# Pauses between GpSimd's pieces, pooled sums behind the key norm, a branch gate multiplied in PSUM, and dense portions around two softmaxes

## The reference

```python
h = rms_norm(x, n1)
z = jnp.einsum('bld,de->ble', h, w_in)
... # o_gla, o_hgrn: chunked linear attention; o_pool: trailing-window means
q = rms_norm(heads(nq, H_D), q_ng)
kv_slc_new = jnp.stack([rms_norm(heads(sk, KVH_D), k_ng[1]), heads(sv, KVH_D)], axis=2)
kv_win_new = jnp.stack([rms_norm(heads(wk, KVH_D), k_ng[2]), heads(wv, KVH_D)], axis=2)
... # NSA: three attentions (compressed, selected, window) with a gate for each
return gb[..., 0:1] * o_cmp + gb[..., 1:2] * o_slc + gb[..., 2:3] * o_win
...
proj = jnp.einsum('blnc,ncd->blnd', branches, w_branch)
gate = jax.nn.sigmoid(jnp.einsum('bld,de->ble', h, w_gate) + b_gate)
x = x + jnp.einsum('bld,de->ble', jnp.sum(gate * proj, axis=2), w_out)
u = jax.nn.relu(jnp.einsum('bld,df->blf', rms_norm(x, n2), w1))
x = x + jnp.einsum('blf,fd->bld', u * u, w2)
```

## Time and profile before

| | us |
|---|---|
| median of 3 runs | 1301.05 |
| lowest and highest | 1300.05, 1306.36 |
| profiled execution, its own time | 1310.57 |
| span in its trace | 1308.7 |
| PE busy | 1225.1 (94%) |
| DVE, POOL, ACT busy | 657.4, 585.0, 345.8 |
| mean granted clock of PE | 0.977 |

### The profile page before, as it was taken

One profiled execution on the slowest core, in us unless ns is written; L12 is line 12 of the kernel. 1 busy time (PEld: TensorE's weight loads), 2 busy tenths in 40 slices (PEclk: granted clock), 3 DMA queues, 4 the chain that ended last, 5 costly groups with the idle time before them and its releaser, 6 DMA issues.

```text
span 1308.7 us, 23691 instructions
## 1 busy us (share of the span) xinstructions
PE 1225.1 (94%) x10261; PEld 1159.6 (89%) x10261; DVE 657.4 (50%) x1036; ACT 345.8 (26%) x516; POOL 585.0 (45%) x433
## 2 busy tenths in 40 slices
PE   4989999999887888899998989989999999999999
PEld 4989899887787778788897988889999999999998
DVE  6244666535475546766755533237387500477200
ACT  5231222210531224333322121223232211222210
POOL 1424566211336338866533434224555544455442
PEclk9999999999998989999998998999999999999999
DMA  4320112123322233434342325142232222233232
GB/s 193 107 72 33 65 66 65 34 69 94 105 65 80 85 113 114 177 114 162 113 156 71 129 85 190 50 146 87 77 113 83 96 97 87 92 97 93 86 97 98
DMA packets 42908, 129.30 MB, mean 99 GB/s; under 512 B 3958, under 2 KB 15006, under 8 KB 40621
## 3 DMA queue, kind: packets, MB, share of 16 engines
q1 hardware_dynamic: 38197, 102.62, 24.1%
q0 software_dynamic: 4608, 25.17, 5.4%
HBM read 121.64 MB, written 6.36 MB: 98 GB/s over the span
## 4 chain that ended last, share of the span: by engine, by line
PE 84%; DVE 9%; DMA 3%; issue 2%; ACT 1%; SPq 0%; POOL 0%; DVEq 0%; ACTq 0%
PE PS L622 20%; PE PS L624 19%; PE PS L623 19%; PE PS L651 9%; PE PS L934 2%; PE PS L727 2%; DMA M<-w_tiles 2%; PE PS L912 2%; PE PS L922 1%; PE PS L1087 1%; DMA M<-state_hgrn 1%; PE PS L763 1%; PE PS L765 1%; DVE stat L1903 1%; PE PS L1079 1%
## 5 line engine op out<-in xcount | busy, mean ns | idle before, releaser
L2195 POOL TENSOR_TENSOR WL<-M,WH 128x512 fp32r<-128x512 f32 x314 | 431.9, 1400 | 647.1 <-ACT WH L1216 646.6
L622 PE MATMUL PS<-hH,WH 128*128 128x260 f32 x1360 | 403.0, 296 | 16.8 <-DVE M L1503 6.6
L624 PE MATMUL PS<-hH,WL 128*128 128x260 f32 x1360 | 389.5, 286 | 0.0
L623 PE MATMUL PS<-hL,WH 128*128 128x260 f32 x1360 | 389.2, 286 | 0.0
L622 PEld LDWEIGHTS PS<-hH,WH 128*128 128x128 f32 x1360 | 261.8, 193 | 32.5 <-issue 27.9
L1216 ACT CAST WH<-M 128x1024 fp32r<-128x1024 f32 x159 | 166.1, 1047 | 378.6 <-DMA M<-w_tiles 243.6
L623 PEld LDWEIGHTS PS<-hL,WH 128*128 128x128 f32 x1360 | 262.2, 193 | 0.4
L624 PEld LDWEIGHTS PS<-hH,WL 128*128 128x128 f32 x1360 | 261.8, 192 | 0.0
L624 PE MATMUL PS<-uH,WL 128*128 128x260 f32 x512 | 144.7, 283 | 0.0
L622 PE MATMUL PS<-uH,WH 128*128 128x260 f32 x512 | 144.6, 282 | 0.0
L623 PE MATMUL PS<-uL,WH 128*128 128x260 f32 x512 | 144.1, 282 | 0.0
(11 more groups left out here) (368 smaller groups left out, 1981.5 us busy)
## 6 DMA issues: line engine op xcount, KB each, us to landing
M<-w_tiles SPq DMA_DIRECT2D x159, 512.0 KB, 3.5
M<-x_T SPq DMA_DIRECT2D x8, 520.0 KB, 5.9
M<-cache_win_kv SPq DMA_DIRECT2D x2, 2048.0 KB, 10.3
y_T<-M SPq DMA_DIRECT2D x8, 260.0 KB
con<-tables SPq DMA_DIRECT2D x1, 1475.5 KB, 12.4
M<-state_gla SPq DMA_DIRECT2D x2, 512.0 KB, 6.6
M<-state_hgrn SPq DMA_DIRECT2D x2, 512.0 KB, 10.4
gla_sample<-M SPq DMA_DIRECT2D x2, 512.0 KB, 6.0
```

The costliest lines, as they stand in the source:

```text
L622: mm(out, hi[:, cols], x_hi, start=first, stop=False)
L623: mm(out, hi[:, cols], x_lo, start=False, stop=False)
L624: return mm(out, lo[:, cols], x_hi, start=False, stop=last_k)
L2195: last = p.tensor_tensor(WL8[s][:, c], WR[s][:, c], WH8[s][:, c], ALU.subtract)
```

## The change

Five things. `lower` on POOL waits for its first piece before it issues the second, and for the second before anything else. The pooled sums begin behind `tick("nsa", 8)` and wait for `k_norm`. In `att` the reciprocal and the gate are no longer multiplied with each other (128x8); the gate is multiplied into PSUM in an instruction of its own (128x512). `cmp` gets three ticks more, 13 of 5, which PE issues behind the scores and ahead of the wait for `cp`. Each softmax round gets a third tick, on PE ahead of the wait for r1, on DVE ahead of the wait for the exponentials. The table pays for it: `att` 3.8 triples in a tick, `s6` 58 ticks of 5.15.

```diff
-SECTIONS = (... ("nsa", 22, 5), ("cmp", 10, 5),
-            ("att", 68, 4), ("s6", 56, 5.4))
+SECTIONS = (... ("nsa", 22, 5), ("cmp", 13, 5),
+            ("att", 68, 3.8), ("s6", 58, 5.15))
...
# PE, compressed scores
                     tick("cmp", 3 + i // 2)
+            for i in range(5, 8):
+                tick("cmp", i)
             pe.wait_ge(*done("cp"))
...
-                tick("cmp", 5 + i)
+                tick("cmp", 8 + i)
...
# PE, sums_of_round
                 tick("s6", at + 1)
+                tick("s6", at + 2)
                 pe.wait_ge(sem("r1"), n + 1)
...
# DVE, compressed softmax
             step(v.tensor_reduce(nmc, cm, AX, ALU.max, negate=True))
+            tick("cmp", 5)
             v.tensor_tensor(cm, cm, bc(nmc, 32), ALU.add).then_inc(once("cm"), 1)
+            tick("cmp", 6)
             dve.wait_ge(*done("cm_e"))
...
+            tick("cmp", 7)
             step(v.reciprocal(rsc, rsc))
...
# DVE, att
                     step(v.reciprocal(rs[:, i, b], rs[:, i, b]))
-                    step(v.tensor_tensor(rs[:, i, b], rs[:, i, b], gate[:, i, :, 1 + b], ALU.mult))
...
                     step(v.tensor_tensor(t, t, bc(rs[:, i, b], HD), ALU.mult))
+                    step(v.tensor_tensor(t, t, bc(gate[:, i, :, 1 + b], HD), ALU.mult))
...
# DVE, softmax_of_round
+                tick("s6", at + 2)
                 dve.wait_ge(sem("sxe"), 2 * n + 2)
...
# POOL, lower
-                    last = p.tensor_tensor(WL8[s][:, c], WR[s][:, c], WH8[s][:, c], ALU.subtract)
-                last.then_inc(sem("w_lo"), 1)
+                    ins = p.tensor_tensor(WL8[s][:, c], WR[s][:, c], WH8[s][:, c], ALU.subtract)
+                    if i == 0:
+                        step(ins)
+                ins.then_inc(sem("w_lo"), 1)
+                gp.wait_ge(sem("w_lo"), n + 1)
...
# POOL, pooled sums
-            for i in range(5):
+            for i in range(9):
                 tick("nsa", i)
+            gp.wait_ge(*done("k_norm"))
             gp.wait_ge(sem("dv"), FREED[U_DONE][1])
```

More of the change, by code:

```diff
@@ L167 @@
 FREED = evacuations()
-SECTIONS = (("prep", 10, 7), ("lev", 32, 7.5), ("dec", 14, 5), ("ssl", 7, 5), ("smp", 24, 5), ("nsa", 22, 5), ("cmp", 10, 5),
-            ("att", 68, 4), ("s6", 56, 5.4))
+SECTIONS = (("prep", 10, 7), ("lev", 32, 7.5), ("dec", 14, 5), ("ssl", 7, 5), ("smp", 24, 5), ("nsa", 22, 5), ("cmp", 13, 5),
+            ("att", 68, 3.8), ("s6", 58, 5.15))
 FIRST, CUM, _sum = {}, [], 0
@@ L585, in _ @@
                              zn[0:NS, 4, col:col + 256]).then_inc(sem("rows_out"), 16)
-            for i in range(10):
+            for i in range(13):
                 tick("cmp", i)
@@ L597, in _ @@
                              [:, 4 * n:4 * n + 4]).then_inc(sem(f"xw{n}"), 16)
-            for i in range(56):
+            for i in range(58):
                 tick("s6", i)
@@ L1055, in _ @@
             sums_of_round(0, SN[1], 28)
-            tick("s6", 30)
+            tick("s6", 31)
             for n in range(2):
@@ L1066, in _ @@
                 last.then_inc(sem("sv_mm"), 4)
-                tick("s6", 31 + n)
+                tick("s6", 32 + n)
             outputs_of_round(0)
-            tick("s6", 33)
+            tick("s6", 34)
             for x in range(NS + 1):
@@ L1089, in _ @@
                     last.then_inc(sem("sx_mm"), 1)
[L1090 to L1093, removed]
+                tick("s6", 35 + x)
+            tick("s6", 44)
+            sums_of_round(1, SN[0], 45)
+            tick("s6", 48)
             pe.wait_ge(sem("snk"), 2)
@@ L1103, in _ @@
                     if i % 4 == 3 and i < 15:
-                        tick("s6", 47 + 4 * n + i // 4)
+                        tick("s6", 49 + 4 * n + i // 4)
                 for k in range(HKV):
@@ L1111, in _ @@
                 last.then_inc(sem("sv_mm"), 4)
-                tick("s6", 50 + 4 * n)
+                tick("s6", 52 + 4 * n)
             outputs_of_round(1)
-            tick("s6", 55)
+            tick("s6", 57)
             assert made[0] == TOTAL and next(more, "end") == "end"
@@ L1389, in _ @@
             f(CM, CM, ACT.Exp).then_inc(once("cm_e"), 1)
-            for i in range(5, 10):
+            for i in range(5, 13):
                 tick("cmp", i)
@@ L1419, in _ @@
             round_exp(0, 1)
-            for i in range(29, 45):
+            for i in range(29, 46):
                 tick("s6", i)
             round_exp(1, 0)
-            for i in range(45, 56):
+            for i in range(46, 58):
                 tick("s6", i)
@@ L2075, in _ @@
                     ins.then_inc(sem("so"), 1)
-            tick("s6", 31)
             tick("s6", 32)
+            tick("s6", 33)
             outputs_of_round(0)
-            tick("s6", 33)
+            tick("s6", 34)
             for x in range(NS + 1):
@@ L2094, in _ @@
                         .then_inc(sem("sx"), 1)
[L2095 to L2098, removed]
+                tick("s6", 35 + x)
+            tick("s6", 44)
+            softmax_of_round(1, 0, 45)
+            tick("s6", 48)
             for x in range(NS):
-                tick("s6", 47 + x)
+                tick("s6", 49 + x)
             dve.wait_ge(sem("sv_mm"), 2 * NS)
@@ L2253, in _ @@
             step(p.tensor_tensor(WP[0][:, :, HIST + 1:], U[:, :, 1:L], U[:, :, 0:L - 1], ALU.add))
-            tick("nsa", 5)
-            tick("nsa", 6)
+            tick("nsa", 9)
+            tick("nsa", 10)
             for n in (1, 2, 3):
@@ L2261, in _ @@
                 step(p.tensor_tensor(dst[:, b:, HIST:], src[:, a:, HIST:], src[:, a:, HIST - sh:HIST + L - sh], ALU.add))
-                tick("nsa", 2 * n + 5)
-                tick("nsa", 2 * n + 6)
+                tick("nsa", 2 * n + 9)
+                tick("nsa", 2 * n + 10)
             for g in range(4):
@@ L2270, in _ @@
                     ins.then_inc(sem("win"), 1)
-            for i in range(13, 22):
+            for i in range(17, 22):
                 tick("nsa", i)
-            for i in range(10):
+            for i in range(13):
                 tick("cmp", i)
@@ L2314, in _ @@
                 keys(x)
-            for i in range(19, 34):
+            for i in range(19, 35):
                 tick("s6", i)
@@ L2324, in _ @@
                 values(4 + x)
-                tick("s6", 34 + x)
-            for i in range(38, 56):
+                tick("s6", 35 + x)
+            for i in range(39, 58):
                 tick("s6", i)
```

## The result

The changed kernel takes 1293.21 us (median of 5 executions, 1292.67 to 1296.11) against 1301.19 for the one before: a ratio of 0.993, 95% interval 0.9911 to 0.9949. It is 8.0 us faster by the medians and 9.1 us by the ratio; forecast were 20.8 us. The direction was right and the size was not: the time lies just inside the range, and under half of the forecast gain is there.

What follows compares the result with a forecast made beforehand. The prediction took PE, busy 94% of the span, as the bound, with only idle time and half-clock stretches to win. Terms summed to 23.2 us, less 2.4 for ACT's casts: 20.8 us, forecast 1280.5 us, range 1270 to 1294.

Steps and rivals of the forecast that it cites:

- compressed softmax: Three ticks fill PE's 6.5 us wait for DVE: 5.4 us go, plus 2.0 of clock, 7.4 us won.
- pooled sums: Sums behind the key norm cut PE's 6.6 us wait to 1.0; with 1.5 of clock, 7.1 us won.
- gate in PSUM: In att, replacing DVE's 6.87 us product removes PE's 4.3 us wait; with 1.5 of clock, 5.8 us won.
- rounds: Sample rounds: second wins 1.8 us plus 1.5 of clock, first loses 0.4; 2.9 us won.
- pauses: Waits between POOL's lowered pieces: taken as 0 us on the path.
- ACT's casts behind late loads: In att, an allowance of 2.4 us lost for one more late load holding ACT's cast.
- the four gaps: PE's idle stretches of 6.6, 6.5, 4.3 and 6.2 us (two rounds), which the change was to shorten.
- The second rival: Att's long gate product was one execution's chance, so 5.8 us are not won: 1286; inside the forecast's 0.56.
- part comes back: Late sums, clock falling behind the softmax gap, two more late ACT casts: 11 us won, about 1290; chance 0.19.
- The prediction's own sign of being wrong: Gaps close without the span following, shown as new PE idle time behind ACT in att.
- The slower rival: ACT becomes the bound in att through casts behind late loads, ending at 1309; chance 0.04.

Runs made afterwards that it cites:

- e2: Kernel before with only the three ticks of 5 triples around the compressed softmax (att 3.8 triples in a tick); ratio 1.0012.
- e11: Changed kernel without the three ticks around the compressed softmax (cmp 10 ticks of 5, att 4 triples in a tick); ratio 0.9903, 1290.6 us.
- e9: Kernel before with the three softmax ticks and DVE's sample parts (query blocks, new keys, diagonal gates) made early between compressed-output steps; ratio 0.9946.
- e3: Kernel before with only the pooled sums moved behind the key norm, without pauses between POOL's pieces; ratio 0.9937.
- e15: Changed kernel with the pooled sums back ahead of the key norm; ratio 1.0008.
- e4: Kernel before with only the gate multiplied in PSUM; ratio 0.9962.
- e13: Changed kernel with the product of 128x8 in place of the gate multiplied in PSUM; ratio 0.9907.
- e6: Kernel before with only the third tick in each softmax round (s6 58 ticks of 5.22 triples); ratio 0.9989.
- e5: Kernel before with only the pauses between POOL's pieces; ratio 0.9966.
- e14: Changed kernel without the pauses between POOL's pieces; ratio 0.9919.
- e1: Kernel before, unchanged, run again for a second trace and the scatter; ratio 0.9992, traced span 1300.3 us.
- e7: Changed kernel with DVE's sample parts (query blocks, new keys, diagonal gates) made early, between the compressed-output steps; ratio 0.9876, 1285.0 us.
- e16: e7 with DVE's third tick of a round behind its last reduction instead of ahead of it; ratio 0.9826, 1281.55 us.
- e8: Changed kernel with ACT casting the tiles loaded in att one tick later; ratio 0.9953.
- e12: e7 with the gathers of cached rows three ticks later in POOL's order; ratio 0.9917.

## Why the prediction was wrong

| step | forecast, us | what the runs showed |
|---|---|---|
| compressed softmax | 7.4 | gap 6.5 to 1.2; worth 0 alone (e2) and in the change (e11), 7.0 with early gates (e9) |
| pooled sums | 7.1 | 8.2 alone (e3); 6.9 up to L855, mean of nine traces with them against nine without; all of the gain when undone (e15) |
| gate in PSUM | 5.8 | 4.9 alone (e4), nothing in company (e13) |
| rounds | 2.9 | 2.7 to 1.0 and 3.5 to 3.9 us as forecast; 1.4 by time (e6) |
| pauses | 0 | 4.4 alone (e5), nothing in company (e14) |
| ACT's casts behind late loads | -2.4 | PE's waits behind ACT 3.0 to 6.5 |
| sum | 20.8 | 8.0 by the medians, 9.1 by the ratio |

**The softmax term failed.** "So 5.4 us go, 1.1 stay" was read rightly from the chain under the gap and is what the trace shows. The step that failed is the next one, by which 5.4 us less at one wait are 5.4 us less at the end. PE came earlier to the first scores of `att`, but DVE's chain, which had set the softmax's end, runs on through the outputs and the sample parts to just that place, and DVE had become slower there (10.07 us for the work of 7.01), beside pieces of POOL's that the same ticks brought. The list of waits of the kernel before holds the sign:

```profile
PE PS L912 <- DVE gaT L1867: 1.0, 1, 1.0
```

PE waited there for DVE even before, 1.0 us, so this place had no slack to take up an earlier arrival. The prediction asked what is late next within the softmax (the bank, the gate on ACT) and stopped at L888.

**The clock was counted as a gain at the four gaps and not as a loss at new ones.** Of the 23.2 us, 1.5 + 2.0 + 1.5 + 1.5 = 6.5 were for the clock. None of it is there: PE's busy time, which a lower clock lengthens, is 1221.7 us in e1 and in the changed kernel alike (1225.1 in the slower first trace), with the same 10261 matmuls, so the 7.6 us by which the spans differ are idle time alone. Stretches went at the old gaps, but new gaps of 2 to 4 us have some behind them; in the changed kernel's `att` PE is busy 6.3 us longer than in e7.

**The gate's term was right alone and is not additive.** The second rival took the 6.87 us for a chance of one execution. It was none (e1), but it was a chance of the alignment: each of the parts that shifted POOL's stream against DVE's there took it away. So the gate's 4.9 and the pauses' 4.4 us pay for the same wait of 4.3 us with its clock. The singles add up to 8.2 + 4.9 + 4.4 + 1.4 - 1.6 = 17.3 us, and the change as a whole has 9.1 by its ratio. With the pauses counted with the gate, and without the ticks, they are 8.2 + 4.9 + 1.4 = 14.5 us, and e11, the change without the ticks, has 12.6 (7.8 to 17.4). There the sum closes; so the shortfall from the forecast lies in the main with the softmax's ticks.

**The sums' term held**: the stage up to L855, which lies ahead of the shared wait, is 6.9 us shorter by the two means, where 7.1 were forecast. They were not late: PE's wait for the pooled products is 1.5 us (1.9 before). The key norm's wait is 2.5 us where 1.0 was forecast. The two copies still took 2.8 us there where the prediction put them at 0.8 each at most, but that is not the whole reason: in e13 they take as long and the wait is 0.9, as in e16. Why is open.

**The rival "part comes back"** is the case that came, with a chance of 0.19, and of its three mechanisms (late sums, clock, casts behind late loads) the last two are in the trace, at other places than named. The main mechanism of what came, the wait for the gates, was not among them. The prediction's own sign of being wrong, that the gaps close and the span does not follow, is what came. The slower rival, ACT as the bound in `att`, did not come: PE's waits behind ACT grew by 3.5 us in all, from 3.0 to 6.5.

**Open** is why gaps of the same length do not always have a half-clock stretch behind them: in e7 idle stretches of 3.1 and 2.1 us in `att` have none, and in the changed kernel those of 3.1 and 2.1 us have. That a load slows down beside a gather is seen, but neither e8 nor e12 turned it into time.

## What to carry to other kernels

Follow the engine that ended the gap past the gap: where its chain runs on to the next wait of the bound engine and that wait is already nearly zero, work moved into the first gap only moves the idle time. Ask of every term whether another part of the change removes the same wait, and count it once. If the next wait can be freed by moving the late engine's small work into its own idle places, as here the gates and the round's tick, the first gain is there.

## What the runs showed of the hardware

A DVE product of two SBUF operands, 0.17 us when free, waited 6.8 us through four back-to-back POOL instructions and a fifth; with a semaphore wait between them, which leaves a gap of 0.08 us on POOL, it got its turn at the end of the running one (1.07 us). A tile load of 512 KB took 8.5 us beside two gathers of 2.1 MB together, 3.6 in the median.
